# Second mixer of a two-block transformer kernel: rotation ahead of the weight splits, one split on GpSimd, other orders around the top-k and in the heads

## The reference

```python
a = rmsnorm_2(h, norm_mix_pre[i]);  u = a @ w_in[i]
q, k, v, qi, ki, wi, u_conv, u_pool = split(u)   # 8 heads of 64, 2 kv heads, 16 index heads of 64
q, k, qi, ki = partial_rope(...)                 # the first 16 of 64 features are rotated
idx = sum_h relu(qi_h . ki) * wi_h * scale       # 256 x 256, causal
sel = top_k(idx, 64)                             # 64 keys for each query
y_attn = softmax(q . k[sel]) @ v[sel]
y_conv = silu(layernorm(conv31(a_half * sigmoid(g_half)) + conv_b)) @ conv_pw
y_pool = (window means of 2, 4, 8, 16 - u_pool) @ pool_w * pool_scale
h = h + rmsnorm_2(concat(y_attn, y_conv, y_pool) @ w_out[i], norm_mix_post[i])
```

## Time and profile before

| | us |
|---|---|
| median of 3 runs | 2012.89 (2012.09 to 2013.71) |
| profiled execution | 2017.22 |
| its span, first to last instruction | 2015.3 |
| TensorE busy | 1933.4 (96%) |
| VectorE busy | 1347.0 (67%) |
| ScalarE busy | 996.5 (49%) |
| GpSimd busy | 241.5 (12%) |
| mean granted TensorE clock | 0.977 |

### The profile page before, as it was taken

One profiled execution on the slowest core, in us unless ns is written; L12 is line 12 of the kernel. 1 busy time (PEld: TensorE's weight loads), 2 busy tenths in 40 slices (PEclk: granted clock), 3 DMA queues, 4 the chain that ended last, 5 costly groups with the idle time before them and its releaser, 6 DMA issues.

```text
span 2015.3 us, 36557 instructions
## 1 busy us (share of the span) xinstructions
PE 1933.4 (96%) x15864; PEld 1913.6 (95%) x15864; DVE 1347.0 (67%) x1605; ACT 996.5 (49%) x1231; POOL 241.5 (12%) x168
## 2 busy tenths in 40 slices
PE   7999999999999999999999999988999998889998
PEld 7999999999999999999999999987999998779998
DVE  6655777775558555787775557886755688675556
ACT  5433545464347444545554446766433476653333
POOL 3000100010002000100010001562100026610000
PEclk8999999999999999999999999979999999789999
DMA  7555454455554655545455554413455543235551
GB/s 260 185 185 184 149 170 159 147 189 188 188 194 146 210 189 190 170 129 167 149 169 201 184 184 155 147 48 126 147 195 182 174 154 106 68 117 203 183 188 64
DMA packets 246531, 329.55 MB, mean 164 GB/s; under 512 B 6246, under 2 KB 218788, under 8 KB 246372
## 3 DMA queue, kind: packets, MB, share of 16 engines
q1 hardware_dynamic: 246018, 326.79, 49.0%
q0 software_dynamic: 96, 0.26, 0.1%
q10 hardware_dynamic: 258, 0.16, 0.1%
HBM read 326.14 MB, written 1.05 MB: 162 GB/s over the span
## 4 chain that ended last, share of the span: by engine, by line
PE 79%; DVE 12%; ACT 4%; POOL 2%; issue 2%; DMA 1%; ACTq 0%; POOLq 0%; DVEq 0%; SPq 0%
PE work L1984 18%; PE work L1985 17%; PE work L1986 17%; PE acc L1986 8%; PE acc L1984 8%; PE acc L1985 8%; DVE w_lo L1300 4%; ACT w_hi L796 1%; POOL fa L743 1%; DVE fa L1732 1%; DVE ra L1313 1%; DVE fa L1345 1%; POOL fa L717 1%; PE work L2111 1%; PE acc L2054 1%
## 5 line engine op out<-in xcount | busy, mean ns | idle before, releaser
L1984 PE MATMUL work<-xh,w_hi 128*128 128x256 f32 x2560 | 724.7, 283 | 24.1 <-DVE xl L1334 12.8
L1300 DVE TENSOR_TENSOR w_lo<-raw,w_hi 128x2048 fp32r<-128x2048 f32 (+2 forms) x314 | 707.1, 2262 | 60.1 <-ACT w_hi L796 58.0
L1985 PE MATMUL work<-xl,w_hi 128*128 128x256 f32 x2560 | 721.6, 282 | 0.0
L1986 PE MATMUL work<-xh,w_lo 128*128 128x256 f32 x2560 | 719.9, 281 | 0.0
L796 ACT ACTIVATE w_hi<-raw 128x2048 fp32r<-128x2048 f32 (+2 forms) x314 | 578.5, 1850 | 168.8 <-PE work L1986 85.8
L1984 PEld LDWEIGHTS work<-xh,w_hi 128*128 128x128 f32 x2560 | 485.9, 190 | 28.1 <-issue 23.9
L1985 PEld LDWEIGHTS work<-xl,w_hi 128*128 128x128 f32 x2560 | 486.4, 190 | 0.4
L1986 PEld LDWEIGHTS work<-xh,w_lo 128*128 128x128 f32 x2560 | 486.3, 190 | 0.0
L1345 DVE TENSOR_TENSOR fa<-work,rstd 128x512 f32<-128x512 f32 x168 | 115.3, 690 | 401.0 <-PE work L1986 400.4
L1984 PE MATMUL acc<-ra,w_hi 128*128 128x256 f32 x1344 | 377.8, 281 | 0.0
L1986 PE MATMUL acc<-ra,w_lo 128*128 128x256 f32 x1344 | 377.4, 281 | 0.0
(11 more groups left out here) (287 smaller groups left out, 2292.0 us busy)
## 6 DMA issues: line engine op xcount, KB each, us to landing
raw<-in_ffn_w_gu_dram SPq DMA_DIRECT2D x88, 1024.0 KB, 5.1
raw<-in_w_in_dram SPq DMA_DIRECT2D x52, 1024.0 KB, 5.4
raw<-in_ffn_w_down_dram SPq DMA_DIRECT2D x44, 1024.0 KB, 5.2
raw<-in_w_up_dram SPq DMA_DIRECT2D x32, 1024.0 KB, 5.5
raw<-in_w_down_dram SPq DMA_DIRECT2D x32, 1024.0 KB, 6.9
raw<-in_w_mla_out_dram SPq DMA_DIRECT2D x8, 1024.0 KB, 5.4
raw<-in_w_o_dram SPq DMA_DIRECT2D x8, 1024.0 KB, 5.1
raw<-in_w_ple_gate_dram SPq DMA_DIRECT2D x8, 1024.0 KB, 5.5
```

The lines of the kernel that those rows point to most:

```text
L1300: v.tensor_tensor(w_lo[:, s, 0:n], raw[:, r, 0:n], w_hi[:, s, 0:n].bitcast(F32), ALU.subtract).then_inc(lo_done.sem, 1)
L1984: pe.matmul(dst, ah, bh, start=start and i == 0, stop=False, skip_group_check=not group)
L1985: pe.matmul(dst, ah, bl, start=False, stop=False, skip_group_check=not group)
L1986: last = pe.matmul(dst, al, bh, start=False, stop=stop and i == len(pairs) - 1, skip_group_check=not group)
```

## The change

Everything is in the second block's mixer; nothing of the computation changes.

- Index loop, VectorE: in turns 2 and 3 the next chunk's split stands behind the rotation instead of at the end of the turn before.
- The split of chunk 10 (Q2 + 1) goes from VectorE, where it stood behind the keys' rotation, to GpSimd, between taps 9 and 10. It waits for the high part of chunk 10 and the low part of chunk 9. VectorE waits for it before chunk 11.
- ScalarE: the relus of index unit 3 come ahead of the copies of values and keys; the keys' high parts ahead of the copy of query unit 0; taps 16 and 17 move behind the second turned query unit, so that four taps stand there.
- Top-k: the values' low part goes from ahead of the last weighted sums into round 1, the rotation of query unit 0 from round 3 to 4, `queries_lo(0)` from 7 to 6, the rotation of query unit 1 from 6 to 7.
- TensorE: the scores of heads 0 and 1 come ahead of the turn of query unit 1; the pool products ahead of head 2's scores; the pool rows' out-projection goes from heads 2 to 5 to heads 1, 2, 3 and 5; in head 6 the output of head 5 comes ahead of the wait for "ota" and the product behind it.
- Heads: the split of chunk 11 (`next_lo(here, P2)`) goes from head 1 to head 0; chunks 13 and 14 go to head 6 on both engines; ScalarE's tap of head 5 comes behind the high part of "ota".

```diff
--- before.py
+++ after.py
@@ -226,10 +226,11 @@
     names += [("qi", 1), ("qit", 1), ("qi", 2), ("qit", 2), ("qi", 3), ("qit", 3), "kv", "pool"]
-    names += [("q", 0), "kt", ("q", 1), ("qt", 0), ("qt", 1), ("sc", 0), ("sc", 1)]
+    names += [("q", 0), "kt", ("q", 1), ("qt", 0), ("sc", 0), ("sc", 1), ("qt", 1)]
     for hd in range(HEADS):
-        names += [("pt", hd)] + ([("sc", hd + 2)] if hd + 2 < HEADS else []) + ([("out", hd - 1)] if hd else [])
-        names += {0: [("poolw", 0), ("poolw", 1)], 5: ["ota"], 6: ["mean"]}.get(hd, [])
+        names += [("pt", hd)] + ([] if hd else [("poolw", 0), ("poolw", 1)])
+        names += ([("sc", hd + 2)] if hd + 2 < HEADS else []) + ([("out", hd - 1)] if hd else [])
+        names += {5: ["ota"], 6: ["mean"]}.get(hd, [])
     names += ["var", ("out", HEADS - 1), "otb", "pw", "mix"]
 ...
@@ -751,6 +752,12 @@
                     tap(j)
+                    if j == TAPS_FIRST - OWN_TAP:
+                        at = CHUNK_AT[here] + Q2 + 1
+                        gp.wait_ge(hi_done.sem, at + 1)
+                        gp.wait_ge(lo_done.sem, at)
+                        gp.tensor_tensor(w_lo[:, at % RING, :], raw[:, at % RAWS, :], w_hi[:, at % RING, :].bitcast(F32),
+                                         ALU.subtract).then_inc(lo_done.sem, 1)
 ...
@@ -1116,6 +1123,7 @@
                 next_hi(here, KV2)
+                relus(3)
                 keys_values = bank2(U2["kv"])
 ...
@@ -1128,7 +1136,6 @@
                 last.then_inc(part_hi.event(here, "kd"), 1)
-                relus(3)
                 next_hi(here, P2)
 ...
@@ -1136,17 +1143,16 @@
                 preload(ACT.Exp)
-                rows_of(("q", 0), "q0", 0)
                 act.wait_ge(*unit_ready.at(here, U2["kt"]))
 ...
                 act.activation(kb[64:128, 0, 0:2, :], bank2(U2["kt"])[64:128, :, :], ACT.Copy).then_inc(part_hi.event(here, "kt"), 1)
-                some_taps(2)
+                rows_of(("q", 0), "q0", 0)
                 hi_of_unit(here, U2["qt", 0], ("qt", 0), qh[:, 0:2, :], bank2(U2["qt", 0]))
 ...
                 hi_of_unit(here, U2["qt", 1], ("qt", 1), qh[:, 2:4, :], bank2(U2["qt", 1]))
-                some_taps(2)
+                some_taps(4)
 ...
@@ -1174,21 +1180,18 @@
                     if hd == 0:
-                        some_taps(1)
                         for k in range(2):
 ...
                         last.then_inc(part_hi.event(here, "pool"), 1)
-                    if hd == 2:
-                        next_hi(here, Q2 + 1)
-                    if hd == 4:
-                        next_hi(here, WO2_POOL)
-                    if 0 < hd < 6:
-                        some_taps(1)
                     if hd == 5:
                         hi_of_unit(here, U2["ota"], "ota", xh[:, 0:2, :], bank2(U2["ota"]))
+                    if hd < 6:
+                        some_taps(1)
                     if hd == 6:
+                        next_hi(here, Q2 + 1)
+                        next_hi(here, WO2_POOL)
                         act.wait_ge(*vec_out.at(here, "centred"))
 ...
@@ -1776,14 +1779,11 @@
                     rope_unit(("qi", c), c)
-                    if c == 1:
-                        next_lo(here, G2_IN)
+                    next_lo(here, QI2[c - 1] if c > 1 else G2_IN)
                     weighted(c - 1)
                     index_queries(c)
-                    next_lo(here, QI2[c])
+                next_lo(here, QI2[3])
                 rope_unit("kv", "kv", 2)
-                next_lo(here, KV2)
-                values_lo()
                 weighted(3)
 ...
@@ -1811,14 +1811,16 @@
                         scaled(here, U2["pool"], pu[:, :, POOL_PAD:])
-                    if r == 3:
+                    if r == 1:
+                        values_lo()
+                    if r == 4:
                         rope_unit(("q", 0), "q0")
 ...
                     if r == 6:
+                        queries_lo(0)
+                    if r == 7:
                         rope_unit(("q", 1), "q1")
-                    if r == 7:
-                        queries_lo(0)
                     chain(here, v.memset(small[:, 26:27], 0.0))
 ...
@@ -1850,19 +1852,18 @@
                                                    xh[:, 6 + k, :].bitcast(F32), ALU.mult, ALU.subtract).then_inc(unit_taken.of(u), 1)
-                    if hd == 1:
+                        v.wait_ge(lo_done.sem, lo_done.after(here, Q2 + 1))
                         next_lo(here, P2)
 ...
                         next_lo(here, Q2)
-                    if hd == 4:
-                        next_lo(here, Q2 + 1)
                     if hd == 5:
                         lo_of_unit(here, U2["ota"], "ota", xl[:, 0:2, :], bank2(U2["ota"]), xh[:, 0:2, :])
+                    if hd == 6:
+                        next_lo(here, Q2 + 1)
                         next_lo(here, WO2_POOL)
-                    if hd == 6:
                         ready(here, U2["mean"])
 ...
@@ -2358,8 +2359,6 @@
                 turned(("qt", 0), tm[:, 0, :, :])
-                pe.wait_ge(*unit_taken.at(here, U2["q", 1]))
-                turned(("qt", 1), tm[:, 1, :, :])
 ...
@@ -2406,23 +2405,11 @@
                 scores(1)
+                pe.wait_ge(*unit_taken.at(here, U2["q", 1]))
+                turned(("qt", 1), tm[:, 1, :, :])
+                pool_rows = (None, 0, 1, 2, None, 3, None, None)
                 for hd in range(HEADS):
                     probs(hd)
-                    if hd + 2 < HEADS:
-                        if hd == 2:
-                            pe.wait_ge(*unit_taken.at(here, U2["qt", 1]))
-                        scores(hd + 2)
-                    if 1 < hd < 6:
-                        if hd == 2:
-                            pe.wait_ge(*dot_taken.at(here, 11))
-                            for k in range(2):
-                                pe.wait_ge(*unit_taken.at(here, U2["poolw", k]))
-                        accumulate(here, WO2_POOL, rows(6), first=True, banks=(hd - 2,))
-                    if hd > 5:
-                        pe.wait_ge(*unit_taken.at(here, U2["ota"]))
-                        accumulate(here, WO2_LOW, rows(0), banks=(hd - 6,))
-                    if hd:
-                        output(hd - 1)
                     if hd == 0:
 ...
@@ -2431,10 +2418,26 @@
                                 unit_ready.sem, 1)
+                    if hd + 2 < HEADS:
+                        if hd == 2:
+                            pe.wait_ge(*unit_taken.at(here, U2["qt", 1]))
+                        scores(hd + 2)
+                    if pool_rows[hd] is not None:
+                        if hd == 1:
+                            pe.wait_ge(*dot_taken.at(here, 11))
+                            for k in range(2):
+                                pe.wait_ge(*unit_taken.at(here, U2["poolw", k]))
+                        accumulate(here, WO2_POOL, rows(6), first=True, banks=(pool_rows[hd],))
+                    if hd == 7:
+                        accumulate(here, WO2_LOW, rows(0), banks=(1,))
+                    if hd:
+                        output(hd - 1)
                     if hd == 5:
 ...
                     if hd == 6:
+                        pe.wait_ge(*unit_taken.at(here, U2["ota"]))
+                        accumulate(here, WO2_LOW, rows(0), banks=(0,))
                         pe.wait_ge(*conv_done.at(here, 0))
 ...
                 pe.wait_ge(*sq_ready.at(here, NB))
```

## The result

The changed kernel takes 2018.93 us (median of 8 runs, 2017.27 to 2022.38), the kernel before 2014.08 beside it (8 runs, 2011.92 to 2017.13). The ratio is 1.0028 with an interval of 1.0018 to 1.0038, which is 3.6 to 7.6 us slower. Forecast were 4.5 us more and 2017.4, with 2009 to 2024.5 as the range.

A forecast was written before the change was run, and what follows sets the result against it. The mixer was taken as bound by turns by VectorE (top-k), latency (first heads) and TensorE. Layer 0's +4.2 and layer 1's +1.3, less 1 for the clock, gave +4.5 on 2012.89: 2017.4 us, range 2009 to 2024.5.

The forecast's parts named there:

- Total: Whole kernel: both layers' terms and the clock's return together cost +4.5 us, giving 2017.4.
- Index loop: Rotation ahead of the split: TensorE's waits of 1.53 and 1.19 go; VectorE's last split ends 1.8 us earlier.
- GpSimd's split: Chunk 10's split on GpSimd takes 4.6 us, and the keys' rotation add on VectorE waits for it.
- Top-k: Mask ready 1 to 1.7 us earlier, but query unit 1's rotation, now last, ends at 1338.4 and 1714.8.
- nothing is gained: VectorE's last weighted sums before the top-k start at 1316.4, against 1316.5 before.
- Four taps: ScalarE's four taps before the first exponential take 4.5 us; it comes 1.3 later in layer 0, 2.3 in layer 1.
- One stated sign of a wrong prediction: Layer 0's first exponential coming before 1344 would show the prediction wrong.
- Another stated sign: The clock in the heads differing from before by more than one 4 us stretch would show the prediction wrong.
- Heads: Head 1 turned 6.5 us after first exponential, about 1 waiting for chunk 11's split; +2.1 in layer 0, +0.4 in layer 1.
- I give back 1 us for a sooner return of the clock in layer 0: Heavy accumulation comes one head earlier, so 1 us is taken off the sum for layer 0's clock.
- Rival (c): Clock stays at 1.2 GHz through one layer's heads: +8 to +14 us, 2025 or more; chance 0.10.
- Mean and variance: After the heads: mean starts 0.2 and 0.9 us earlier; mean to variance changes by +1.0 and −0.5.

The follow-up runs named there:

- experiment 1: Changed kernel with ScalarE's taps 19 and 20 moved behind the exponentials of heads 0 and 1: 2015.51 us, ratio 1.0016 to the kernel before.
- Experiments 2 and 3: Changed kernel with chunk 10's split back on VectorE behind the keys' rotation: 2021.02 us; changed kernel with GpSimd's split waiting for that rotation: 2020.16 us.
- Experiment 5: Changed kernel, taps 19 and 20 behind first two exponentials, GpSimd's split behind keys' rotation, layer 0's pool unit scaled two top-k rounds later: 2011.32 us.
- experiment 7: Changed kernel with everything from the first exponential on as in the kernel before: 2016.13 us, ratio 1.0011 to the kernel before.
- experiment 12: Experiment 5 plus repeated TensorE products in three waits ahead of the first head, in free banks: 2009.73 us, ratio 0.9980 to the kernel before.
- the two parts put back alone: Changed kernel with pool products behind head 2's scores again: ratio 1.0019; with head 5's tap and the splits of chunks 13 and 14 as before: 1.0044.

## Why the prediction was right

**Total.** +4.5 was forecast and +5.6 (3.6 to 7.6) measured; the two profiled mixers give +4.5. The single layers were 3 us off each in opposite ways (+0.3 for +3.2, +4.2 for +1.3), so the total owes a good part to luck. That the profiled mixers give the very number is luck too: those of experiment 1 are 1.7 longer than the changed kernel's where the timed runs are 2.4 shorter.

**Index loop: right.** TensorE's waits of 1.53 and 1.19 are gone; the largest that is left is 0.28 in layer 0 and 0.30 in layer 1. VectorE's last split ends at mixer time 29.83 (30.2 forecast).

**GpSimd's split: right in mechanism and size** (4.51 and 4.60 against 4.6; the add 4.39 and 4.46). One reading behind it was off: the add of 0.23 that was set against one of 1.16 is the keys' of 64 elements, while the slow one has 128 (0.46 in the changed kernel's row at 1334.39). The lock stands all the same. Experiments 2 and 3 showed that without the other edits the lock cost no time that could be measured, which the prediction did not say: in layer 0 the pool unit was next, and then the taps. Experiment 5 shows that with the taps moved it does.

**Top-k.** Query unit 1's rotation ended at 56.3 in both layers, and 57.2 and 57.1 were forecast. It is 0.8 early because the last sums were 0.8 early, where "nothing is gained" had been written.

**Four taps: right, 4.50 for 4.5** (the items given for it add up to 4.7). With that 0.8, and in layer 0 ScalarE's 2.2 where 2.5 was taken (2.6 in layer 1), the first exponential is 1.2 and 0.6 earlier than forecast: +0.06 for +1.3, +1.66 for +2.3. That is the mis-sized term of the front. One stated sign of a wrong prediction is an exponential of layer 0 before 1344. It stands at 1341.5 in the changed profile, and at 1344.2 when the start of the mixer is put on that of before, which is the fair comparison. Another stated sign, a clock in the heads that differs from before by more than one stretch of 4 us, did come, in both layers.

**Heads.** Head 1 at 6.31 for 6.5, the split's wait 0.94 for about 1, both right in both layers. The step that failed is the clock's: "I give back 1 us for a sooner return of the clock in layer 0", and nothing for layer 1. In layer 0 it returned at mixer time 75 (82 before), in layer 1 at 82 (68 before), and the stretches moved the same way, -1.43 and +2.35 where +0.9 and -0.5 were forecast. Within the changed kernel the clock is worth 2.96: same waits, a return 7 us later. In the old heads it is worth less: experiment 7 has 34.20 with a return at 82 and 33.26 with a return at 68, as the waits grow when the clock is up (for the split of chunk 11 from 0.30 to 1.80). So of the -1.43 and the +2.35 the share of the clock and that of the new order are not separated. Over two layers the time at 1.2 GHz between first exponential and mean did not change (32 us before, 31 now). Rival (c), the clock low through one layer's heads, came in part, in layer 1, at about a quarter of its price.

**Mean and variance.** The convolution is done 5.1 after ScalarE begins on the turned output (5.4 forecast), and the mean waits 2.12 for it. The variance then comes 5.26 later for 4.6. At the full clock it comes after 4.02 (experiments 5 and 12, one layer and both): so the two splits cost 0.4 and not 1.0, and the rest is the clock, which is at 1.2 GHz for some 3 us right behind the mean's start. The wait alone does not bring that about: of the 15 mixers with a wait of 2.08 to 2.12 there, ten have it and five do not (both of experiment 12).

**Open.** Why the new heads cost 3.4 us by experiment 7, while of the two parts put back alone one gives 1.8 (its interval reaches to nothing gained) and the other a loss. In the two profiles 3.3 of their 4.6 us lie between mean and variance. The order of the out-projection's pool rows and the place of chunk 11's split were not tried alone. The mean clock over one stretch differs by up to 0.2 between profiles of nearly the same code, one profile was taken of each, and the runs do not settle it.

## What to carry to other kernels

Before giving an instruction to an idle engine, look at what that engine will exclude: GpSimd had the 4.5 us to spare, but the 0.2 us add behind them paid for it with 4.2; waiting for that one add puts the split beside work that it does not disturb. Where several chains end within a few us of each other (here the sums, the pool unit, the taps and the maxima), an edit alone shows little or a loss, and only the set of them moves the time: -2.4 and +2.2 alone, -6.8 together with the pool unit's. And where TensorE stands for some us ahead of small, dependent work, price the clock with the wait: filling three waits with thrown-away products came with some 2.8 us less than the best version here (intervals overlap).

## What the runs showed of the hardware

- GpSimd's subtraction of 128 x 2048 took 4.51 to 4.63 us in every trace, and held a 64-element VectorE add for all but 0.2 of it; eight VectorE sums with an operand in PSUM ran beside it in 3.80, as without it. The Trainium skill (GPSIMD Engine Reference, Elementwise — side-by-side cycle accounting) measures 4497 ns for a float32 tensor_tensor of 2048 elements, which agrees.
- After a drop, the return of the clock varied: it came between mixer time 68 and 83 in 23 of the 28 profiled mixers (in the other five first at 61 to 65, to fall again), and hardly with where the heads began (75 with a first exponential at 57.05 and at 62.95). In the changed kernel TensorE has the same waits behind the first exponential in both layers, and the returns at 75 and 82 set the stretches 2.96 us apart. So one profile of a stretch that holds a drop says little to within 3 us, and the timed runs of one kernel spread over up to 8 us.
